# A two-block fp32 layer stack on one core: the weight sums of a seven-product matrix multiplication made by accumulating transfers

## The reference, cut to what matters

```python
def swiglu(x, w_gate, w_up, w_down):
    return (jax.nn.silu(x @ w_gate) * (x @ w_up)) @ w_down

x = layer_norm(ALPHA * x + 0.5 * swiglu(...), g, b)   # twice a layer, as the kernel scales it
```

## Time and profile before

| | |
|---|---|
| median of 3 runs | 2987.71 us (2985.76 to 2988.74) |
| the profiled execution | 2987.91 us, of which the traced span is 2986.0 us |
| PE busy (matmul) | 2866.7 us, 96% |
| DVE, ACT, POOL busy | 1625.3, 1097.3, 83.7 us |
| HBM read | 277.82 MB |
| TensorE clock granted, mean | 0.99 |

### The profile page before, as it was taken

How to read it: one execution, slowest core, us unless ns; L and a number is a source line. 1 busy time by engine, 2 the same in 40 slices (tenths; PEclk the granted TensorE clock), 3 DMA queues, 4 the chain that set the end, 5 groups by cost and what they waited for, 6 DMA issues and landing times.

```text
span 2986.0 us, 34129 instructions
## 1 busy us (share of the span) xinstructions
PE 2866.7 (96%) x14401; PEld 2381.4 (80%) x14401; DVE 1625.3 (54%) x2227; ACT 1097.3 (37%) x1416; POOL 83.7 (3%) x91
## 2 busy tenths in 40 slices
PE   7999998999999989999999999999999999999998
PEld 7888877887888878878876888888787886787887
DVE  4345357734635665563556484635746364656455
ACT  4322443432234333332535532324333354543332
POOL 0020000001000000000100000000000010000000
PEclk9999999999999999999999999999999999999999
DMA  5242122223221122333521233232332341232322
GB/s 203 80 131 77 65 78 78 97 71 113 78 78 59 69 93 99 113 113 105 100 94 57 85 127 127 85 111 73 128 127 98 102 98 57 75 123 99 113 99 85
DMA packets 59112, 288.41 MB, mean 97 GB/s; under 512 B 6404, under 2 KB 6594, under 8 KB 31312
## 3 DMA queue, kind: packets, MB, share of 16 engines
q1 hardware_dynamic: 53216, 263.21, 25.6%
q0 software_dynamic: 4288, 15.22, 2.4%
q10 hardware_dynamic: 1456, 7.80, 0.9%
HBM read 277.82 MB, written 2.10 MB: 94 GB/s over the span
## 4 chain that ended last, share of the span: by engine, by line
PE 78%; DVE 12%; ACT 4%; DMA 3%; issue 2%; ACTq 0%; SPq 0%; DVEq 0%
PE G L473 15%; PE G L475 15%; PE G L474 15%; PE G L485 7%; PE G L487 7%; PE G L486 7%; DMA raw<-in_stream 2%; DVE w_lo L1660 2%; DVE w_lo L2291 2%; PE G L947 1%; ACT w_hi L1455 1%; PE G L948 1%; PE G L949 1%; ACT w_hi L1108 1%; PE A L998 1%
## 5 line engine op out<-in xcount | busy, mean ns | idle before, releaser
L473 PE MATMUL G<-xT_hi,w_hi 128*128 128x512 f32 (+1 forms) x2368 | 881.5, 372 | 16.5 <-DVE x L2217 5.3
L475 PE MATMUL G<-xT_hi,w_lo 128*128 128x512 f32 (+1 forms) x2368 | 870.2, 367 | 0.0
L474 PE MATMUL G<-xT_lo,w_hi 128*128 128x512 f32 (+1 forms) x2368 | 869.8, 367 | 0.0
L1660 DVE TENSOR_TENSOR w_lo<-raw,w_hi 128x2048 fp32r<-128x2048 f32 (+1 forms) x210 | 480.0, 2286 | 512.6 <-ACT w_hi L1108 512.3
L1108 ACT ACTIVATE w_hi<-raw 128x2048 fp32r<-128x2048 f32 (+1 forms) x210 | 397.9, 1895 | 713.6 <-PE G L475 376.6
L473 PEld LDWEIGHTS G<-xT_hi,w_hi 128*128 128x128 f32 x2368 | 449.2, 190 | 89.3 <-DVE x L2217 5.9
L475 PEld LDWEIGHTS G<-xT_hi,w_lo 128*128 128x128 f32 x2368 | 449.0, 190 | 73.5
L474 PEld LDWEIGHTS G<-xT_lo,w_hi 128*128 128x128 f32 x2368 | 449.7, 190 | 68.8
L485 PE MATMUL G<-w_hi,xT_hi 128*128 128x512 f32 (+1 forms) x512 | 194.7, 380 | 9.4 <-DVE w_lo L1660 4.0
L947 PE MATMUL G<-w_hi,hs 128*128 128x512 f32 x448 | 178.0, 397 | 14.8 <-DVE w_lo L2291 14.8
L487 PE MATMUL G<-w_hi,xT_lo 128*128 128x512 f32 (+1 forms) x512 | 187.2, 366 | 0.0
(11 more groups left out here) (316 smaller groups left out, 3661.0 us busy)
## 6 DMA issues: line engine op xcount, KB each, us to landing
raw<-in_stream SPq DMA_DIRECT2D x208, 1024.0 KB, 4.9
raw<-in_stream SPq DMA_DIRECT2D x80, 512.0 KB, 6.2
lnr<-in_ln_rows POOLq DMA_DIRECT2D x6, 1024.0 KB, 5.2
row<-in_rows POOLq DMA_DIRECT2D x6, 512.0 KB, 7.0
x<-in_x ACTq DMA_DIRECT2D x1, 2048.0 KB, 17.9
tB<-fA ACTq DMA_DIRECT2D x4, 512.0 KB, 5.4
xn<-fB ACTq DMA_DIRECT2D x4, 512.0 KB, 8.4
shift_t<-work POOLq DMA_DIRECT2D x32, 62.0 KB, 11.7
```

The source lines that it names most:

```text
L473: mm(o, a, hi[:, c, at:at + n], start=start and own_start, stop=False, **k)
L474: mm(o, a, lo[:, c, at:at + n], start=False, stop=False, **k)
L475: return mm(o, wl[:, col:col + P], hi[:, c, at:at + n], start=False, stop=stop, **k)
L1660: tt(w_lo[:, s, 0:nk, :], raw[:, r, 0:nk, :], w_hi[:, s, 0:nk, :].bitcast(F32), ALU.subtract).then_inc(lo_done, 1)
```

## The change

1. The sums of weights are no longer made by DVE. SP loads six quarters (B22 to `raw2[:, 0]`, B11 to `raw2[:, 1]`, before the seventh block of the part; then B11, B11, B21, B12 through the ring `raw`). GpSimd adds five more onto them with transfers that accumulate (`accum_op=ALU.add`), each pair of 512 KB behind the semaphore of what it adds to: z = B11 + B12, then + B22, in `raw2[:, 1]`; y = B11 + B12 in `raw[:, 1]`; later B12 + B22 in `raw[:, 1]`, and z + B21.
2. The products come in another order, with other signs and banks. A product that adds to an earlier one of the same banks has to wait until DVE has read that one (`SAME_BANKS`): k=2 behind k=1, k=6 behind k=5.
3. In `ffn` on ACT and DVE the seven hidden operands are made in another order, and `read_product` of k=1 is cut in its two tiles around a low part.
4. In the layer norm (`ahead`), the first tile is measured and scaled ahead of the low part; ACT's second half of the bias rows comes behind the high part of the next weight block.

```diff
 SP, feed_forward
                     for i in range(2 * units):
+                        if n < SUMMED and i == 6:
+                            if parts_before + n == 0:
+                                sp.wait_ge(S["ln_c"], 1)
+                            down = b + 2 * units
+                            alternate(raw2[:, 0], down + 2, 1, (raw2_in[0], raw2_in[0]))
+                            alternate(raw2[:, 1], down, 0, (raw2_in[1], raw2_in[1]))
                         ring(b + i)
...
                     alternate(raw[:, 0], b, 0, (half_in[0], raw_in[0]))
+                    taken(first)
+                    slot_free()
+                    alternate(raw[:, 1], b, 0, (y_in, raw_in[1]))
+                    taken(first + 1)
+                    slot_free()
+                    alternate(raw[:, 0], b, 1, (half_in[0], raw_in[0]))
                     taken(first + 4)
                     slot_free()
-                    alternate(raw[:, 1], b + 2, 0, (half_in[1], raw_in[1]))
-                    taken(first + 3)
-                    sp.wait_ge(lo_done, first + 2 + 3)
-                    sp.wait_ge(S["w_sum"], 4 * (parts_before + n) + 4)
-                    alternate(raw2[:, 0], b + 2, 1, (raw2_in[0], raw2_in[0]))
+                    alternate(raw[:, 1], b + 2, 0, (y_in, raw_in[1]))
+                    taken(first + 5)
 ACT, ffn, the last unit of a part
-                                act.wait_ge(raw2_in[1], 32 * (N.parts + 1))
-                                split_summed(raw2[:, 1])
+                                act.wait_ge(y_sum, 64 * N.parts + 32)
+                                split()
 ACT, layer_norm
                 if ahead:
                     split(ahead=1)
+                if bias_rows:
+                    bias_rows(1)
 DVE, layer_norm
-                if ahead:
-                    split()
                 for t in (0, 1):
                     measured(t, scale, eps)
                     scaled(t)
+                    if ahead and t == 0:
+                        split()
 DVE: first_weight_sum to fourth_weight_sum and their calls are gone
 GpSimd
+            def add_from(place, b, odd, signal):
+                for o in range(2):
+                    pool.dma_start(place[:, 2 * o:2 * o + 2, :],
+                                   stream[b + o:b + o + 1].rearrange("o p (k e n) -> (o p) k e n", e=2, n=BC)[:, :, odd, :],
+                                   accum_op=ALU.add).then_inc(signal, 16)
+            def sums_of_weights(l, f, part):
...
+                pool.wait_ge(raw2_in[1], 32 * p + 32)
+                add_from(raw2[:, 1], b + 2, 0, z_sum)
+                pool.wait_ge(z_sum, 96 * p + 32)
+                add_from(raw2[:, 1], b + 2, 1, z_sum)
+                pool.wait_ge(y_in, 32 * p + 16)
+                pool.wait_ge(raw_in[1], (ring // 2 + 1) * 16)
+                add_from(raw[:, 1], b + 2, 0, y_sum)
+                pool.wait_ge(y_in, 32 * p + 32)
+                pool.wait_ge(raw_in[1], (ring // 2 + 2) * 16)
+                add_from(raw[:, 1], b + 2, 1, y_sum)
+                pool.wait_ge(z_sum, 96 * p + 64)
+                pool.wait_ge(lo_done, split + 6)
+                add_from(raw2[:, 1], b, 1, z_sum)
...
                 load_ln(0)
...
+                sums_of_weights(l, 0, 0)
+                sums_of_weights(l, 0, 1)
...
                 pool.wait_ge(S["x_res"], 4 * (3 * l + 2))
                 load_ln(2)
+                sums_of_weights(l, 1, 0)
+                sums_of_weights(l, 1, 1)
```

More of the change, by code:

```diff
@@ L943, in products @@
                             if i == 0:
-                                pe.wait_ge(S["ff_lo"], N.ff + 3 * u + min(k, 2) + 1)
+                                pe.wait_ge(S["ff_lo"], N.ff + 3 * u + (1 if k == 0 else 2 if k < 4 else 3))
                             hi, lo = (hs[:, u, part, LEFT[k], i * P:i * P + P] for part in range(2))
-                            new, end = u == 0 and k in (0, 1, 3), u == units - 1
+                            new, end = u == 0 and k in (0, 1, 4), u == units - 1
                             mm(o, hi, w_hi[:, s, u, :], start=new, stop=False, skip_group_check=True)
@@ L1501, in ffn @@
                     if n < SUMMED:
[L1502 to L1505, removed]
+                        act.wait_ge(raw2_in[0], 32 * (N.parts + 1))
                         split_summed(raw2[:, 0])
-                        act.wait_ge(S["w_sum"], 4 * N.parts + 4)
+                        act.wait_ge(z_sum, 96 * N.parts + 64)
                         split_summed(raw2[:, 1])
+                        Pos.fewer += 2
+                        act.wait_ge(half_in[0], 16 * (2 * N.parts + 2))
+                        split()
+                        act.wait_ge(y_sum, 64 * N.parts + 64)
+                        split()
+                        act.wait_ge(z_sum, 96 * N.parts + 96)
+                        split_summed(raw2[:, 1])
+                        Pos.fewer += 1
                         N.parts += 1
-                        Pos.fewer += PRODUCTS - 2
                         split()
@@ L2307, in sums_of_h, with read_product @@
                 tt(s3, h11, h21, ALU.subtract)
[L2308 to L2335, removed]
+                link(tt(s1, h22, h21, ALU.subtract))
+                link(stt(out=s2, in0=s1, scalar=-1.0, in1=h11, op0=ALU.mult, op1=ALU.subtract))
+                stt(out=s4, in0=s2, scalar=-1.0, in1=h12, op0=ALU.mult, op1=ALU.subtract).then_inc(S["ff_sum"], 1)
+            def read_product(k, n, tiles=(0, 1), blocks_ahead=0):
                 half, col = QUARTER[k]
-                for i in range(2):
+                op = ALU.add if SIGN[k] > 0 else ALU.subtract
+                for i in tiles:
                     if i == 0:
@@ L2341, in read_product @@
                     else:
-                        dve.wait_ge(blk_used, 2 * Pos.pair + Pos.end + k + (3 if k == 0 else 1))
-                    if k in (1, 4):
-                        dve.wait_ge(S["st_read"], 2 * (PRODUCTS * N.parts + k - 1) + i + 1)
+                        dve.wait_ge(blk_used, 2 * Pos.pair + Pos.end + blocks_ahead + k + 1)
+                    if SAME_QUARTER[k] is not None:
+                        dve.wait_ge(S["st_read"], 2 * (PRODUCTS * N.parts + SAME_QUARTER[k]) + i + 1)
                     o = x[:, 2 * half + i, col * 512:col * 512 + 512]
-                    g = G[:, 2 * (k % 2) + i, :]
-                    if n == 0 and k in (0, 2, 3, 6):
-                        ins = stt(out=o, in0=o, scalar=2.0 * ALPHA, in1=g, op0=ALU.mult, op1=ALU.add)
+                    g = G[:, BANKS[k] + i, :]
+                    if n == 0 and SAME_QUARTER[k] is None:
+                        ins = stt(out=o, in0=o, scalar=2.0 * ALPHA, in1=g, op0=ALU.mult, op1=op)
                     else:
-                        ins = tt(o, o, g, ALU.add)
+                        ins = tt(o, o, g, op)
                     ins.then_inc(S["st_read"], 1)
@@ L2396, in ffn @@
                     if n < SUMMED:
[L2397 to L2400, removed]
+                        split_summed(raw2[:, 1])
+                        Pos.fewer += 2
                         read_product(2, n)
-                        split_summed(raw[:, 0])
+                        split()
                         read_product(3, n)
-                        split_summed(raw2[:, 0])
+                        split()
                         read_product(4, n)
                         split_summed(raw2[:, 1])
-                        Pos.fewer += PRODUCTS - 2
+                        Pos.fewer += 1
                         read_product(5, n)
```

68 lines of the change are left out of this document (35 added, 33 removed).

## The result

The changed kernel takes 3057.82 us (median of 4 runs, 3055.71 to 3061.97) against 2988.22 us of the kernel before on the same chip: ratio 1.0235 (95% interval 1.0219 to 1.0250). The profiled execution took 3057.71 us, its span is 3055.9. So +69.8 us on the profiled time of 2987.91, where +30 was forecast.

The account below looks back on a forecast made before the run. PE, busy 96% of the span, was taken as the bound, so only its waits cost time. Product waits -14.8, norm -6.5, late stages +47.7, clock +3.6 gave +30.0 on 2987.91: 3018 us, range 2976 to 3058.

Parts of the forecast that it names:

- PE's waits for L2291: Product stages: 14.8 us in 16 PE waits for low parts, two a stage, to go with DVE's sums; gain 14.8 us.
- shared banks: Product 2 waiting for DVE's reading of product 1's first tile: taken as 0; as a rival, products 1 and 5, +6 us.
- The norm: Layer norm: with the first tile measured earlier, PE's waits for ACT's norm shrink by 6.5 of 7.8 us.
- y is just in time: Ordinary stages: y's addition 9.1 us plus high and low part 4.3 exactly fill the 13.4 us before product 1.
- five ordinary stages: The stages other than 1761, 2125 and 2706: sums of weights land in time, so no PE wait, 0 us.
- The price of an addition: Accumulating pair of 512 KB issued by GpSimd: 9.1 us from issue to landing, each further queued pair 5.8; bounds 6.2 and 12.4.
- The three late stages: Stages of 1761, 2125, 2706: GpSimd issues z late, y queues behind; PE waits 47.7 us before product 1, some 16 each.
- Clock: After the three long PE waits: a lower granted clock costs 1.8 us each, 5.4 less the one already there, +3.6.
- all eight stages wait: Rival, product stages: adding pairs take 12 us or more, y is late everywhere, 3059 us and above; chance 0.20.

Follow-up runs that it names:

- both repairs: Changed kernel with y made by DVE and z's additions issued ahead of GpSimd's wait for x_res: 2961.92 us against 2988.11 of the kernel before, ratio 0.9915.

## Why the prediction was wrong

**Right in mechanism.** What it named decided the sign: GpSimd works in order, in three stages it stands at another wait when z is due, and y is queued behind both of z's additions. The three waits before product 1, at the forecast stages, are 59.9 us, and moving the issue took 47.9 of them away. PE's waits for L2291 went, HBM reads rose by 50.3 MB (50 forecast), no wait for shared banks came. The norm gained 6.8 us of waits (6.5 forecast), DVE's busy time fell by 63.4 us (73 forecast, 32 sums of 2.29); the sums were there in full, 73.2 us by their own durations, and the page counts less because DVE's instructions overlap.

**The step that failed: "y is just in time", five ordinary stages at 0.** It set the addition's 9.1 us and 4.3 for both parts against 13.4 between the landing of the direct part and product 1. Measured, as means over the five: 0.54 us until GpSimd issues, 11.8 to ACT's split (11.46 to 12.51), 4.3 for both parts, against 12.4 of room (11.5 to 13.0, since the same load now starts 17.3 to 18.3 us before product 1 and not 18.9). 16.6 less 12.4 is 4.2 us, five times 21.1. A sum that comes out at exactly nothing has no margin, and three small terms went against it: the wake-up that GpSimd needs at each link (0.5), the addition itself (2.7, of which 2.2 is SP's next load, issued within 0.9 us of it, as holding it back showed), and the room (1.0). The price of an addition, 9.1, was nearly right where z's first pair shows it in these stages: 9.6 to the landing, 9.9 to the next issue.

**The three late stages: 47.7 forecast, 59.9 measured.** Chains of 98.2 us in sum from z's issue in place of 87.9, with 38.3 of room in place of 40.2. z's second and y's additions take 14.6 us together (14.9 forecast). z's first takes 13.1, 14.7 and 13.6 us (9.1 forecast, and 1 for `load_ln`). Over those stretches the engines are 0.88 to 0.96 busy, with SP's weight loads and the row of 1 MB that GpSimd issues 0.6 us ahead; which of them counts for how much was not tried apart.

```profile
1757.00:1770.00 13.00, 13.00 (x59) 10.75 (x58) 5.08 (x8) 1.62 (x3) 2.57 (x3) 1.00 0.88 239
...
2749.00:2762.00 13.00, 13.00 (x58) 10.51 (x56) 4.56 (x8) 1.21 (x3) 2.05 (x2) 1.00 0.96 241
```

**Clock: +3.6 forecast, +8.9 measured** as PE's busy time. The step that failed here: the loss was given to the three long waits alone, one of 1.8 us each. Each of the eight waits is followed by 1.7 to 3.1 us lost in product 1 (7.15 to 8.49 us from its first matmul to the next product's, in place of 5.44), 19.1 us in all. The products' matmuls are busy for 314.2 us before, 326.4 in the changed kernel and 306.9 in the one with both repairs: that puts some 7 us of clock on the old waits before products 3 and 5, which the forecast had not credited. The other matmuls are busy for 3.3 us less, which stays unexplained.

**The account.** Waits of products +66.2 (33 forecast: 47.7 - 14.8), norm -6.8 (-6.5), one block +1.3 (0), clock +8.9 (+3.6): 69.6 of the 69.8 us. Of the 40 us that the forecast lacked, 21.1 are the five ordinary stages, 12.2 the three late ones and 5.3 the clock. The rival "all eight stages wait", from pairs of 12 us or more, given 0.20 and 3059 us, is what happened: from the landing of y's direct part to ACT's split it is 12.4 us where it matters.

## What to carry to other kernels

A sum moved from an engine with room to a transfer trades 2.3 us of hidden work for a chain link of 10 to 12 us; it pays only where that link has more room than this, with the queue's wake-up and the neighbours' traffic counted. Before giving an in-order queue new work, list what it is waiting for at the moment when the work is due: here that alone cost 48 us in three stages, and a call moved ahead of a wait in each took it back. Where a term comes out as "just in time", price it as late by the spread of its parts, and use an engine's spare time for the one operand that is due first.

## What the runs showed of the hardware that was not expected

- GpSimd is occupied for 2.2 us by issuing a pair of adding transfers of 512 KB and for 1.45 by a plain pair of the same shape. One plain transfer takes 0.72 us of it; adding ones take 1.1 to 1.5 and overlap.
- An adding transfer moves in packets of half the size (2048 bytes and not 4096) that take as long, 0.192 us, so it costs the 16 engines twice the time of a plain one, 2.9 us more a MB. A pair of 512 KB takes 3.3 us longer (9.9 against 6.5 until GpSimd issues the next). Four queued adding transfers alone kept the engines 89% busy over 14 us.
- What a wait costs beside itself does not follow from its length. Product 1 took 5.83 us after waits of 1.33 and 1.84 us but 7.46 after one of 1.83, 7.44 after 2.46, 7.41 after 19.33 and 8.75 after 3.27, in place of 5.70.
